# Eleven modulation blocks of a two-block diffusion transformer, taken from TensorE to ScalarE and GpSimd

## The reference, cut to what matters

```python
def adaln(cond, w, b):
    m = jax.nn.silu(cond) @ w + b
    return jnp.split(m[:, None, :], 6, axis=-1)

for i in range(DEPTH):        # DEPTH = 2; the third matrix belongs to the block behind
    ...                       # attention, residual with gate
    x = x + g2 * squared_relu_mlp(modulate(rms_norm(x, norm_mlp[i]), sh2, sc2), mlp_w1[i], mlp_w2[i])

def squared_relu_mlp(h, w1, w2):
    return jnp.square(jax.nn.relu(h @ w1)) @ w2
```

## Time and profile before

| | us |
|---|---|
| median of 3 runs | 1795.95 (1789.97 to 1797.92) |
| profiled execution: its own time | 1786.23 |
| profiled execution: span of the trace | 1784.4 |
| TensorE busy in the span | 1705.8 (96%) |
| VectorE busy | 992.8 (56%) |
| ScalarE busy | 694.3 (39%) |
| GpSimd busy | 138.0 (8%) |

### The profile page before, as it was taken

One profiled execution on the slowest core, in us unless ns is written; L12 is line 12 of the kernel. 1 busy time (PEld: TensorE's weight loads), 2 busy tenths in 40 slices (PEclk: granted clock), 3 DMA queues, 4 the chain that ended last, 5 costly groups with the idle time before them and its releaser, 6 DMA issues.

```text
span 1784.4 us, 26580 instructions
## 1 busy us (share of the span) xinstructions
PE 1705.8 (96%) x10450; PEld 1365.5 (77%) x10450; DVE 992.8 (56%) x1796; ACT 694.3 (39%) x1255; POOL 138.0 (8%) x146
## 2 busy tenths in 40 slices
PE   5999998999999999999999999999999899999997
PEld 2775446778888887454689999777689799989997
DVE  3445865643434343345836666676588855555454
ACT  3333655332323232234635444543310166344443
POOL 1020000100000001033000000100124000200000
PEclk9999999999999999999999999999999999999999
DMA  9225991222222223343034444233130334435342
GB/s 406 83 95 227 364 353 42 101 95 95 95 94 95 95 95 115 130 177 154 36 141 188 181 171 178 89 142 142 48 142 2 142 142 147 180 146 189 145 160 74
DMA packets 21323, 254.02 MB, mean 142 GB/s; under 512 B 2256, under 2 KB 4560, under 8 KB 5584
## 3 DMA queue, kind: packets, MB, share of 16 engines
q1 hardware_dynamic: 18144, 242.51, 35.6%
q10 hardware_dynamic: 3056, 9.82, 1.5%
HBM read 251.26 MB, written 1.05 MB: 141 GB/s over the span
## 4 chain that ended last, share of the span: by engine, by line
PE 81%; DVE 10%; ACT 4%; issue 2%; DMA 1%; POOL 1%; DVEq 0%; POOLq 0%; SPq 0%; ACTq 0%
PE bank L550 18%; PE bank L551 17%; PE bank L552 17%; PE bank L507 10%; PE bank L998 4%; PE bank L607 3%; PE bank L686 2%; DVE w_lo L1729 2%; PE bank L712 2%; PE bank L694 2%; ACT w_hi L1271 1%; DMA weights<-in_ada 1%; DVE root L1593 1%; DVE slab L1705 1%; PE bank L661 1%
## 5 line engine op out<-in xcount | busy, mean ns | idle before, releaser
L1729 DVE TENSOR_TENSOR w_lo<-weights,w_hi 128x1024 fp32r<-128x1024 f32 (+2 forms) x286 | 331.8, 1169 | 110.0 <-ACT w_hi L1271 107.2
L1271 ACT ACTIVATE w_hi<-weights 128x1024 fp32r<-128x1024 f32 (+2 forms) x286 | 287.7, 1013 | 231.7 <-PE bank L552 227.4
L550 PE MATMUL bank<-h_hi,w_hi 128*128 128x256 f32 (+1 forms) x1024 | 338.9, 331 | 14.2 <-DVE w_lo L1729 7.8
L552 PE MATMUL bank<-h_hi,w_lo 128*128 128x256 f32 (+1 forms) x1024 | 336.2, 328 | 0.0
L551 PE MATMUL bank<-h_lo,w_hi 128*128 128x256 f32 (+1 forms) x960 | 311.8, 325 | 0.0
L550 PEld LDWEIGHTS bank<-h_hi,w_hi 128*128 128x128 f32 x1024 | 193.1, 189 | 41.4 <-issue 19.5
L552 PEld LDWEIGHTS bank<-h_hi,w_lo 128*128 128x128 f32 x1024 | 192.5, 188 | 18.7
L551 PEld LDWEIGHTS bank<-h_lo,w_hi 128*128 128x128 f32 x960 | 181.2, 189 | 15.4
L551 PE MATMUL bank<-mlp_hidden_lo,w_hi 128*128 128x512 f32 (+1 forms) x512 | 174.6, 341 | 0.0
L550 PE MATMUL bank<-mlp_hidden_hi,w_hi 128*128 128x512 f32 (+1 forms) x512 | 173.1, 338 | 0.6 <-DVE w_lo L1729 0.6
L552 PE MATMUL bank<-mlp_hidden_hi,w_lo 128*128 128x512 f32 (+1 forms) x512 | 172.7, 337 | 0.0
(11 more groups left out here) (274 smaller groups left out, 2816.7 us busy)
## 6 DMA issues: line engine op xcount, KB each, us to landing
weights<-in_ada SPq DMA_DIRECT2D x36, 2048.0 KB, 9.5
weights<-in_mlp_up SPq DMA_DIRECT2D x16, 2048.0 KB, 8.1
weights<-in_mlp_down SPq DMA_DIRECT2D x16, 2048.0 KB, 8.0
weights<-in_ffn_in SPq DMA_DIRECT2D x11, 2048.0 KB, 8.0
weights<-in_in SPq DMA_DIRECT2D x8, 2048.0 KB, 7.9
weights<-in_gate SPq DMA_DIRECT2D x6, 2048.0 KB, 8.0
weights<-in_ffn_out SPq DMA_DIRECT2D x8, 1408.0 KB, 6.0
weights<-in_even_in SPq DMA_DIRECT2D x3, 2048.0 KB, 11.0
```

What stands on the lines that cost most here:

```text
L550: mm(b[:, 0:width], wh, hi(k), start=k == 0, stop=False)
L552: return mm(b[:, 0:width], wl, hi(k), start=False, stop=k == kc - 1)
L1271: A(split_part(w_hi, q), raw_part(q), ACT.Copy).then_inc(sem("w_hi_ready"), 1)
L1729: V.tensor_tensor(split_part(w_lo, q), raw_part(q), split_part(w_hi, q).bitcast(F32), ALU.subtract)\
```

## The change

Of the 18 ada blocks in the attention 8 stay, at pairs 0, 3, ..., 21. Ten of them, and the one in the norm ahead of the first MLP (where four filler matmuls now stand), become 11 "pooled" blocks, which are batch 2 now. Their weights enter the ring between the blocks of the first MLP (`ada_ask`, ahead of m = 2 to 12). ScalarE multiplies each of a block's eight 128 x 512 pieces by the condition, for both sides: 16 products (`ada_products`), four ahead of the split in each of the MLP groups 4 to 47. GpSimd adds them up in pairs of sides: 14 adds for each block. TensorE then sums over the partitions with a tile of ones and zeros (`pick`), two matmuls of 512 columns for each block (`ada_pooled`, ahead of m = 4, 6, ..., 14). Product `a` waits until add `a-4` is complete, since there are four temporaries. The fold of batch 1 moves from pair 11 to pair 23, that of batch 2 from pair 25 to ahead of m = 15.

```diff
-        ADA_BATCHES = [[(0, 0, 4)], [(0, 4, 12)], [(1, 0, 10)], [(1, 10, 12), (2, 0, 6)], [(2, 6, 12)]]
+        ADA_BATCHES = [[(0, 0, 4)], [(0, 4, 12)], [(1, 0, 11)], [(1, 11, 12), (2, 0, 6)], [(2, 6, 12)]]
...
-        ADA_START, ADA_ATT = 4, 18
-        ada_steps = [7 * j // 5 for j in range(ADA_ATT)]
-        ada_ended = {"even": {ada_steps[ADA_ENDS[batch] - ADA_START - 1]: batch for batch in (1, 2)}, "odd": {8: 3}}
+        ADA_START, ADA_ATT, ADA_POOL = 4, 8, 11
+        ada_steps = [3 * j for j in range(ADA_ATT)]
+        ada_sums = [arena[:, at:at + 1024].rearrange("p (s c) -> p s c", s=SIDES) for at in (13824, 14848, 15872)] + [sq]
+        ada_tmp = [arena[:, 16896:17408], arena[:, 17408:17920], root[:, 0, :], root[:, 1, :]]
+        ADA_ADDS = SIDES * (DC - 1)
...
+            def ada_ask():
+
+                j = len(pool_blocks)
+                _, n, blk = ADA_ORDER[ADA_ENDS[1] + j]
+                pool_blocks.append(len(stream))
+                stream.append([f"ada{n}", blk, ("ada_product", SIDES * DC * (j + 1))])
+
+            def ada_pooled(count):
+
+                batch, _, _ = ADA_ORDER[ada[0]]
+                j = ada[0] - ADA_ENDS[1]
+                pe.wait_ge(sem("ada_sum"), ADA_ADDS * (j + count))
+                if j == 0:
+                    pe.wait_ge(sem("ada_copied"), batch)
+                for j in range(j, j + count):
+                    for s in range(SIDES):
+                        at = (2 * (j % 2) + s) * ADA_WIDE
+                        row = SIDES * j + s
+                        ins = mm(banks[ADA_BANK][at:at + ADA_WIDE, :],
+                                 pick[:, ADA_WIDE - 1 - row:2 * ADA_WIDE - 1 - row],
+                                 ada_sums[j % 4][:, s, :], start=j < 2, stop=j >= ADA_POOL - 2)
+                    ins.then_inc(sem("ada_used"), 1)
+                ada[0] += count
+
+            def ada_aside():
+
+                m = mlp0_block[0]
+                mlp0_block[0] += 1
+                if 2 <= m < 2 + ADA_POOL:
+                    ada_ask()
+                if 4 <= m < 4 + ADA_POOL and m % 2 == 0:
+                    ada_pooled(min(2, ADA_ENDS[2] - ada[0]))
+                if m == 15:
+                    ada_fold(2)
...
-            norm("mlp0", TOK)
+            norm("mlp0", TOK, False, 4)
...
+            def ada_products(j, k0):
+
+                n = pool_blocks[j]
+                act.wait_ge(weights_in[n % RING], 16 * (n // RING + 1))
+                if k0 == 0 and j >= 4:
+                    act.wait_ge(sem("ada_used"), ADA_ENDS[1] + j - 3)
+                w = ring[n % RING][:, 0:DC * 512].rearrange("p (k c) -> p k c", c=512)
+                for k in (k0, k0 + 1):
+                    for s in range(SIDES):
+                        a = ADA_ADDS * j + SIDES * (k - 1) + s
+                        if k and a >= 4:
+                            act.wait_ge(sem("ada_sum"), a - 3)
+                        at = ADA_WIDE - SIDES + s
+                        A(ada_tmp[a % 4] if k else ada_sums[j % 4][:, s, :], w[:, k, :], ACT.Copy,
+                          scale=cond[:, 0, k, at:at + 1]).then_inc(sem("ada_product"), 1)
...
+                    if name == "mlp0" and at == 56:
+                        ada_copy(2)
+                    if name == "mlp0" and 4 <= at < 4 + 4 * ADA_POOL:
+                        ada_products(at // 4 - 1, 2 * (at % 4))
...
+            for j in range(ADA_POOL):
+                for k in range(1, DC):
+                    for s in range(SIDES):
+                        a = ADA_ADDS * j + SIDES * (k - 1) + s
+                        pool.wait_ge(sem("ada_product"), SIDES * (DC * j + k) + s + 1)
+                        if k > 1:
+                            pool.wait_ge(sem("ada_sum"), a - SIDES + 1)
+                        nc.gpsimd.tensor_tensor(ada_sums[j % 4][:, s, :], ada_sums[j % 4][:, s, :], ada_tmp[a % 4],
+                                                ALU.add).then_inc(sem("ada_sum"), 1)
```

More of the change, by code:

```diff
@@ L29 @@
 RING = 3
-ARENA = 24300
+ARENA = 24232
 GRID = 64
@@ L416, in build @@
         ADA_ENDS = [sum(ADA_SIZES[:batch + 1]) for batch in range(len(ADA_BATCHES))]
-        ADA_START, ADA_ATT = 4, 18
-        ada_steps = [7 * j // 5 for j in range(ADA_ATT)]
-        ada_ended = {"even": {ada_steps[ADA_ENDS[batch] - ADA_START - 1]: batch for batch in (1, 2)}, "odd": {8: 3}}
+        ADA_START, ADA_ATT, ADA_POOL = 4, 8, 11
[3 more added lines that the diff above has]
+        ADA_ADDS = SIDES * (DC - 1)
+        pool_blocks = []
+        ada_ended = {"even": {ada_steps[ADA_ENDS[batch] - ADA_START - 1]: batch for batch in (1,)}, "odd": {8: 3}}
         def even_items():
@@ L538, in part_used, with split_linear @@
                 parts[-1][3] = used[0]
-            def split_linear(name, blocks, hi, lo, width, tag, before=None, lead=False, after=None, idle=(0, 0)):
+            def split_linear(name, blocks, hi, lo, width, tag, before=None, lead=False, after=None, idle=(0, 0),
+                             front=None):
                 rows, cols, _ = WEIGHTS[name]
@@ L554, in split_linear @@
                 for blk in blocks:
+                    if front:
+                        front()
                     stream.append([name, blk, None])
@@ L733, in up @@
                                  (lambda k, m: pe.wait_ge(sem(f"mlp{n}_h"), k + 1) if m == 0 else None) if q == 0
-                                 else None, lead=q == 0, idle=idle)
+                                 else None, lead=q == 0, idle=idle, front=None if n else ada_aside)
                 def down(q):
@@ L738, in down @@
                                  lambda k: lo[:, (8 * q + k) % keep, :], width, lambda m: (f"mlp_down{n}", 8 * q + m),
-                                 lambda k, m: pe.wait_ge(sem(f"mlp{n}_hid"), 8 * q + k + 1) if m == 0 else None)
+                                 lambda k, m: pe.wait_ge(sem(f"mlp{n}_hid"), 8 * q + k + 1) if m == 0 else None,
+                                 front=None if n else ada_aside)
                 for step, q in MLP_ORDER[n]:
@@ L1157, in _ @@
                         sp.wait_ge(sem("w_lo_ready"), last)
-                    elif last[0] == "ada_used":
-                        sp.wait_ge(sem("ada_used"), last[1])
+                    elif last[0] in ("ada_used", "ada_product"):
+                        sp.wait_ge(sem(last[0]), last[1])
                     else:
@@ L1766, in rest @@
                         .then_inc(sem(f"{name}_hid"), 1)
-                for step, i in mlp_groups(name):
+                for at, (step, i) in enumerate(mlp_groups(name)):
+                    if name == "mlp0" and at == 60:
+                        ada_bias(2)
                     if step == "up":
```

6 lines of the change are left out of this document (5 added, 1 removed).

## The result

| | us |
|---|---|
| before, median of 20 runs | 1791.64 (1786.1 to 1797.92) |
| changed, median of 20 runs | 1795.82 (1789.91 to 1799.78) |
| ratio | 1.0023, 95% interval 1.0013 to 1.0034 |
| changed, profiled execution and its span | 1795.45, 1793.7 |

The account below looks back on a forecast made before the run. TensorE was taken as the bound, except in the attention's first 16 pairs, where VectorE's work limits the gain. Attention -12.2, norm 0, MLP calls and fold +6.5, stalls +1.5: -4.2 us from 1795.95 gives 1791.8 us; range 1783 to 1805.

Parts of the forecast that it names:

- The attention's first 16 pairs: Attention, pairs 0 to 15: TensorE loses 12.2 us of work, but only VectorE's waits can go, 5.2 us gained.
- The floor: Attention, pairs 0 to 15: VectorE's rows and links need about 60 of the 65 us.
- the half clock: Attention: the forecast would be wrong if TensorE's clock fell below the granted 1.00 as it idles more; no size given.
- Pairs 16 to 27: Later attention, bounded by TensorE: four blocks less free 7.4 us, taken as 7.0; with the first 16 pairs 12.2 us.
- The forecast of 100 us up to pair 28: Attention: the stage up to pair 28 should take about 100 us in place of 112.4.
- the attention gives back less: Rival, attention: only 8 us come back as waits for exponentials take back a third; 1796 us, chance 12%.
- The norm: Ahead of the first MLP: an ada block of 1.86 us goes, four fillers of 1.8 us come; zero change.
- The MLP: First MLP: pooled calls and the fold of batch 2 add 6.5 us on TensorE's path, stalls 1.5 us.
- The calls: First MLP: six `ada_pooled` calls on TensorE, five of 0.93 us and one of 0.9, 5.5 us in sum.
- The stalls: First MLP: GpSimd just keeps up with TensorE, and 1.5 us is lost to its delays; bounds 0 and 18 us.
- GpSimd's pace sets the MLP: Rival, MLP: each add keeps 1.41 us, stalls make 18 us; 1808.2 us, slower, chance 14%.
- the turns cost in full: Rival, MLP: GpSimd and VectorE exclude each other without overlap, 263.1 us, 9 us of stalls; 1799.3 us, chance 20%.

Follow-up runs that it names:

- early6: Changed kernel with its first six ada blocks at pairs 0, 1, 2, 4, 5, 7, the late two still at 18 and 21: 1792.76 us, ratio 1.0003.
- gap_fill: Changed kernel plus five zero-weight matmuls at each of four places in pairs 2, 3 and 14 of the attention: 1793.18 us, ratio 1.0004.
- early8: Changed kernel with all eight ada blocks in the first 16 pairs, at 0, 1, 2, 4, 6, 8, 11, 14: 1793.98 us, ratio 1.0007.
- step4: Changed kernel with the ada block of pair 3 moved to pair 4, the others unmoved: 1801.8 us, a single execution.
- bare: Changed kernel with batch 1's eight blocks left out of the attention, a token matmul each instead: 1784.58 us, a single execution.
- hold: Changed kernel plus three zero-weight matmuls in each of pairs 2 to 15: 1794.69 us, ratio 1.0018.
- hybrid12: Changed kernel with twelve ada blocks at the kernel before's places in the first 16 pairs, none after, seven pooled: 1786.06 us, ratio 0.9978.
- bare_hold: Changed kernel without batch 1's eight blocks (token matmuls instead), plus three zero-weight matmuls in each of pairs 3 to 14: 1791.84 us, a single execution.
- att_alone: Changed kernel without the pooled blocks' products, adds, transfers and sums, only a token 8-column matmul for each block: 1787.76 us, ratio 0.9971.
- filled: Changed kernel with eight ada blocks at the kernel before's first eight places and zero-weight matmuls at the ten others: 1802.67 us, ratio 1.0053.
- hold_early8: Changed kernel with ada blocks at 0, 1, 2, 4, 6, 8, 11, 14 and three zero-weight matmuls in pairs 3 to 14: 1791.43 us, ratio 0.9994.

## Why the prediction was wrong

**The attention's first 16 pairs: the step that failed.** "So the stage can shrink only by VectorE's waits, 3.5 + 0.5 + 1.3 = 5.3 us, and I take 5.2": it grew by 0.8. These 6.0 us are most of the 8.4 between forecast and result (1.2 more came from pairs 16 to 27, 1.5 from the MLP, and the norm gave 0.3 back). The floor was right: VectorE needs about 59.5 us besides its waits (table below). The window of the earlier trace rows ends just ahead of a further wait of 1.7 us, for the scores of pair 16, so there were 7.0 us of waits and not 5.3. What the best of the kernels gave back is 4.0 us (early6) rather than 5.2. But I took all of them for six blocks fewer, wherever the six that stay stand. The change also moved those that stay, from 0, 1, 2, 4, 5, 7 to 0, 3, 6, 9, 12, 15, and the prediction never priced a place. The block at pair 3 puts 1.9 us ahead of the scores that VectorE is about to ask for; the trace shows a wait of 4.1 us. Early6, with the same work at the old places, gives back 4.0 us. That one choice costs 4.8 us in the profiled executions, more than the whole loss at the end.

VectorE's waits account for the stage: what is left without them is nearly the same in every kernel. Times in us, up to VectorE's first maximum of pair 16, counted from the first scores; "fold" is the wait for the fold of batch 1, and a wait of 0.4 us for the very first scores, which all have, is left out:

| kernel | waits, by the pair waited for | sum | maximum of pair 16 | less the waits |
|---|---|---|---|---|
| before | 4: 0.8, 5: 0.7, 8: 1.5, fold 1.3, 12: 0.2, 15: 0.5, 16: 1.7 | 6.7 | 66.4 | 59.7 |
| changed | 4: 4.1, 7: 1.7, 15: 0.2, 16: 1.7 | 7.8 | 67.2 | 59.4 |
| gap_fill | 4: 2.7, 7: 3.4, 16: 1.3 | 7.4 | 66.8 | 59.4 |
| early8 | 4: 0.8, 5: 0.7, 7: 4.7, 11: 0.2, 12: 1.2, 15: 1.9 | 9.5 | 68.8 | 59.3 |
| step4 | 4: 2.9, 5: 0.7, 7: 3.3, 16: 1.8 | 8.6 | 68.2 | 59.6 |
| bare | 4: 3.1, 15: 0.7 | 3.8 | 63.2 | 59.5 |
| early6 | 4: 0.8, 5: 0.7, 8: 1.5 | 3.0 | 62.4 | 59.4 |

The changed kernel's 7.8 us of waits against early6's 3.0 are the 4.8 us. At pair 4 the block and the half clock have 1.9 and 1.5 us of them; at pair 16, right behind the block of pair 15, it is 1.7.

**What I first took for the cause** was the half clock, which the prediction named only as something that would upset it. It came (two stretches, 6.8 us) but the attention of hold, without it, was only 0.9 us shorter, and early6 keeps 6.8 us of it and loses nothing by it, since VectorE does not wait for scores where it stands. At pair 3 it adds 1.5 us to the wait for scores, since there the transposes are what VectorE waits behind. That the block at pair 3 alone is the cause fell too (step4): the loss moved on to pairs 4 to 7. A spacing of three pairs is not bad throughout: the blocks at 0, 9 and 12 have no wait behind them, those at 3, 6 and 15 have. What sets the one sort of place apart, and what brings the half clock where it comes, is open.

**Pairs 16 to 27.** 7.0 us forecast, 5.8 measured for four blocks, 1.45 each; hybrid12 has 1.55 each for six. TensorE's waits for exponentials take back a fifth, somewhat more than I allowed. Together: -5.0 us where the sum had -12.2. The forecast of 100 us up to pair 28 is what bare_hold needs, with no block at all (100.2); the changed kernel takes 107.4. The rival "the attention gives back less" was the nearest, but its reason (waits for exponentials take back a third) fits only this stage, and it was still too mild (-8).

**The norm.** Zero forecast, -0.3 measured.

**The MLP.** 8.0 us forecast, 9.5 measured. The calls are the term that was mis-sized: five of 0.93 and one of 0.9, 5.5 us in sum, came to 7.2, 1.2 each. With the fold (1.0 forecast, 0.9 measured) that is 8.0 us, the upper bound ("if each call has to drain the array first"); that a call pays for the interruption is shown by att_alone (0.43 us with next to nothing in it), that it is a draining of the array is not. The stalls (1.5) measure 0.9: TensorE's row is held up once, with a wait of 0.70 us for w_lo. About 0.6 us of the 9.5 has no row.

**What held.** GpSimd: 247.1 us of adds forecast, 245.5 measured, with adds at 1.30 us alone, 1.25 us from start to start (1.27 forecast), and 2.28 us long where w_lo falls in. ScalarE's products are hidden (its waits for GpSimd sum to 39 us, and TensorE's row is held up by 0.9 us), and so are the transfers (7.8 us to land in the median, against 9.5 in the earlier trace rows). So "GpSimd's pace sets the MLP" and "the turns cost in full" both fell. The latter is the rule of the Trainium skill (SBUF — State Buffer, "Who interferes with whom") at its word: 263 us by this case's durations. The trace agrees with its mechanism, and with the 0.25 us of overlap in each turn that the earlier trace rows show and the page does not have.

**The clock between runs.** Over the 35 runs of the kernel before in one comparison, the time falls by 1.5 us for each 0.001 of granted clock, and from 0.989 to 0.997 this makes 12 of its spread of 13 us. By estimate one stretch of 3.4 us at half clock lowers the mean over 1790 us by 0.001, so this is the price of a stretch at 0.43 us for each microsecond (filled). On such lines, one for each kernel's own runs, the times at a clock of 0.995 are: before 1789, changed 1791, early8 1788, hybrid12 1786. So a part of the changed kernel's 4.2 us (about 1.3 remain by these lines) comes with a lower clock, 0.9915 in the median against 0.9925 to 0.993 of the kernel before in the later comparisons; whether its idling causes that was not settled.

## What to carry to other kernels

When work is taken from an engine that two others wait for, price the places of what stays, not only how much goes: name at each place what the second engine asks for next. Measure first with the work left out altogether: here the first 16 pairs hold twelve blocks for 4.0 us more than that (0.33 each, and six of them, at the right places, for nothing that shows) while the later pairs pay 1.55 each and the MLP 0.87. Then add up the second engine's waits, one by one: what is left is its own chain, the same in every variant. That points straight at hybrid12: move only what stands where the engine is the bound. And a short burst put in a dense row of matmuls pays for the interruption as well as for itself.

## What the runs showed of the hardware

- Two matmuls of 8 columns onto a strip of 32 columns, in a row of full-size matmuls, cost 0.43 us (att_alone); four of 512 columns on four strips cost 1.20, and two on two strips 1.18 (changed kernel).
- TensorE's clock fell to half (0.50, 1.2 GHz) in stretches inside the attention in most of the kernels in which it idles more, and not in the two executions with TensorE's work as before in the first 16 pairs (before, hybrid12) nor in hold and hold_early8. It also fell once with the work put back (filled), so idling is not the whole of it.
- A microsecond at half clock costs 0.43 us where VectorE waits for TensorE's scores (filled, 2.9 / 6.8; at pair 3 of the changed kernel 1.5 / 3.4), and nothing that shows where it does not (early6).
- An add of 128 x 512 on GpSimd takes 1.30 us alone and 2.28 us where VectorE's w_lo, with both operands in SBUF, runs beside it; w_lo takes 1.22 us alone and 2.31 beside adds (changed kernel).
